# Other sizes for the weight units of the first down product's second half, and a later place for the first S5 factors

## The reference

```python
def swiglu(x, w1, w3, w2):
    return (jax.nn.silu(x @ w1) * (x @ w3)) @ w2

def s5_mixer(u, lam_re, lam_im, log_dt, b_re, b_im, c_re, c_im, d_skip, w_glu, b_glu):
    ...
    bb_re = f_re[..., None] * br - f_im[..., None] * bi
    bb_im = f_re[..., None] * bi + f_im[..., None] * br
    ...

def first_block(...):
    h = x
    for i in range(DEPTH):
        h = layer_norm(DN_ALPHA * h + 0.5 * swiglu(h, ffn_w1[i, 0], ffn_w3[i, 0], ffn_w2[i, 0]),
                       ln_g[i, 0], ln_b[i, 0])
        ...
```

## Time and profile before

| | |
|---|---|
| median of three runs | 2871.54 us |
| profiled execution, its own time | 2872.73 us |
| its span | 2870.9 us |
| TensorE (PE) busy | 2792.7 us, 97% of the span |
| VectorE (DVE) busy | 1769.1 us, 62% |
| GpSimd (POOL) busy | 314.7 us, 11% |
| mean granted TensorE clock | 0.993 |
| TensorE's waits from 255 to 425 us | 1.8 us for VectorE's L966 (once), 0.6 for its L971 (once), 1.3 for its L1832 (once), 0.5 for ScalarE's L618 (twice), 0.4 for ScalarE's L789 (once) |

### The profile page before, as it was taken

The page is one execution under the profiler, slowest core; times in us unless marked ns, Lnnn a source line. Parts: engine busy times, 40 slices in busy tenths (PEclk is TensorE's granted clock), DMA queues, the critical chain, the costliest instruction groups (busy, mean ns, idle before and its releaser), DMA issues.

```text
span 2870.9 us, 34110 instructions
## 1 busy us (share of the span) xinstructions
PE 2792.7 (97%) x13330; PEld 2142.1 (75%) x13330; DVE 1769.1 (62%) x3753; ACT 623.6 (22%) x1360; POOL 314.7 (11%) x301
## 2 busy tenths in 40 slices
PE   9999999999999999999999999999999999999985
PEld 6888887668888877888855577888877766885321
DVE  4788688775755475566348866677356445664223
ACT  1322120022221021221022422222022463001001
POOL 0000020020000100000101430000100473001221
PEclk9999999999999999999999999999999999999998
DMA  4323333112313222133211111232223201257998
GB/s 171 118 103 125 129 125 111 70 59 88 118 67 132 88 88 88 59 118 116 95 71 59 45 59 62 86 118 100 98 74 109 90 16 59 88 238 280 423 425 326
DMA packets 63716, 351.20 MB, mean 122 GB/s; under 512 B 8238, under 2 KB 14510, under 8 KB 24768
## 3 DMA queue, kind: packets, MB, share of 16 engines
q1 hardware_dynamic: 45792, 320.88, 29.1%
q10 hardware_dynamic: 12896, 19.68, 2.0%
q0 software_dynamic: 4864, 8.40, 0.8%
HBM read 339.49 MB, written 14.16 MB: 123 GB/s over the span
## 4 chain that ended last, share of the span: by engine, by line
PE 89%; DVE 4%; SPq 3%; ACT 1%; DMA 1%; issue 1%; ACTq 0%; POOL 0%; DVEq 0%; POOLq 0%
PE bank L944 33%; PE bank L1142 31%; PE bank L542 6%; PE bank L551 5%; SPq L3953 3%; PE bank L4015 2%; PE bank L2836 2%; PE bank L580 2%; PE bank L3441 2%; PE bank L2820 1%; DMA ring<-in_weights 1%; PE bank L4034 1%; PE bank L572 1%; PE bank L685 1%; PE bank L3065 0%
## 5 line engine op out<-in xcount | busy, mean ns | idle before, releaser
L944 PE MATMUL bank<-area,mixed 128*128 128x256 f32 x2264 | 508.4, 379 | 2.4 <-DVE mixed L966 1.8
L944 PEld LDWEIGHTS bank<-area,mixed 128*128 128x128 f32 x2264 | 429.8, 190 | 61.9 <-DVE mixed L966 2.5
L944 PE MATMUL bank<-area,ring 128*128 128x256 f32 x1536 | 346.3, 379 | 0.1
L1142 PE MATMUL bank<-area 128*128 128x256 f32 x1440 | 323.9, 379 | 0.0
L944 PEld LDWEIGHTS bank<-area,ring 128*128 128x128 f32 x1536 | 291.5, 190 | 40.2 <-DVE area L985 0.5
L1142 PEld LDWEIGHTS bank<-area 128*128 128x128 f32 x1440 | 273.7, 190 | 37.1
L1142 PE MATMUL bank<-buf_b,area 128*128 128x256 f32 x1040 | 239.3, 379 | 0.0
L1142 PE MATMUL bank<-buf_a,area 128*128 128x256 f32 x1040 | 239.2, 379 | 0.0
L1142 PEld LDWEIGHTS bank<-buf_b,area 128*128 128x128 f32 x1040 | 197.6, 190 | 27.0 <-issue 0.3
L1142 PEld LDWEIGHTS bank<-buf_a,area 128*128 128x128 f32 x1040 | 197.7, 190 | 26.8
L966 DVE TENSOR_TENSOR mixed<-ring 128x512 f32<-128x512 f32 (+2 forms) x95 | 64.9, 684 | 226.4 <-PE bank L944 226.1
(11 more groups left out here) (645 smaller groups left out, 4345.5 us busy)
## 6 DMA issues: line engine op xcount, KB each, us to landing
ring<-in_weights SPq DMA_DIRECT2D x236, 1024.0 KB, 4.8
area<-in_weights SPq DMA_DIRECT2D x35, 1024.0 KB, 27.9
buf_b<-in_weights SPq DMA_DIRECT2D x10, 1024.0 KB, 26.3
buf_a<-in_weights SPq DMA_DIRECT2D x8, 1024.0 KB, 24.6
const<-in_weights SPq DMA_DIRECT2D x5, 1024.0 KB, 27.9
norm<-in_weights SPq DMA_DIRECT2D x4, 1024.0 KB, 22.4
mixed<-in_weights SPq DMA_DIRECT2D x4, 1024.0 KB, 26.4
area<-area ACTq DMA_DIRECT2D x20, 128.0 KB, 2.4
```

What stands on the lines that cost most here:

```text
L944: mm = pe.e.matmul(b, w[:, k * P:(k + 1) * P], x(INPUT_OF[p], unit.lo + k), start=(unit.key, BANK_OF[p]) not in begun, stop=unit.last and ...
L1142: mm = pe.e.matmul(out[:, half * H:(half + 1) * H], weights[:, at:at + P], x(name, d), start=fresh and half == 0 and d == 0, stop=half == ...
```

## The change

`SECOND_FIRST` = 1 is new. In the second half of the first down (products 4 to 7), the five pairs are cut into a unit of one pair and then one of four, in place of four and then one. `groups_of` gives the cut, `square` lays the weights out in that order, `place_pieces` starts a new block behind the unit of one pair, and `Unit` and `plan_units` read the cut from `groups_of`. A product of the second half takes two blocks of the ring as before. Besides this, `vector_s5_b(ve, 0)` moves from ahead of the loop to behind the weight sums of unit (0, 1).

```diff
--- before.py
+++ after.py
@@ -65,7 +65,7 @@
 ROUTED = 8 + NEXP
 EARLY_QUERIES = 1
 GROUP = 4
-FIRST_PAIRS = 6
+FIRST_PAIRS, SECOND_FIRST = 6, 1
 WIDE_FFN, WIDE_GROUPS = (0, 1, 2, 3), 5
 SQUARE = ("ffn0_wide", "ffn1_wide", "ffn2_wide", "ffn3_wide", "ffn0_down", "ab_hu", "ffn1_down", "ffn2_down", "ffn3_down",
           "ab_out", "ple0_gate", "c_out", "ple1_gate", "b_merge", "b_out",
@@ -90,15 +90,20 @@
     return ((k * P, P),)
 
 
-def square(name, index, outs, ins, rows=whole, cols=whole):
+def groups_of(n, first=GROUP):
+
+    return [(0, min(first, n))] + [(lo, min(lo + GROUP, n)) for lo in range(first, n, GROUP)]
+
+
+def square(name, index, outs, ins, rows=whole, cols=whole, first_group=GROUP):
 
 
     products = []
     for first, second in outs:
         pieces = []
-        for lo in range(0, len(ins), GROUP):
+        for lo, hi in groups_of(len(ins), first_group):
             for out, side in ((first, 0), (second, 0), (first, 1), (second, 1)):
-                pieces += [(name, index, rows(pair[side]), cols(out)) for pair in ins[lo:lo + GROUP]]
+                pieces += [(name, index, rows(pair[side]), cols(out)) for pair in ins[lo:hi]]
         products.append(pieces)
     return products
 
@@ -125,7 +130,7 @@
     wide = [(2 * c + 1, 2 * c) for c in range(KF // 2)]
     outs = [(2 * c + 1, 2 * c) for c in range(KD // 2)]
     if (layer, i) == (0, 0):
-        return square("ffn_w2", (layer, i), outs, wide[:FIRST_PAIRS]) + square("ffn_w2", (layer, i), outs, wide[FIRST_PAIRS:])
+        return square("ffn_w2", (layer, i), outs, wide[:FIRST_PAIRS]) + square("ffn_w2", (layer, i), outs, wide[FIRST_PAIRS:], first_group=SECOND_FIRST)
     return square("ffn_w2", (layer, i), outs, wide)
 
 
@@ -236,8 +241,11 @@
 def place_pieces(plan):
 
 
-    places, block, col, last = [], 0, 0, (None, 0)
+    places, block, col, last, n_taken = [], 0, 0, (None, 0), 0
     for (name, m), piece in in_order(plan):
+        n_taken = n_taken + 1 if last == (name, m) else 0
+        if name == "ffn0_down" and m >= KD // 2 and n_taken == 4 * SECOND_FIRST:
+            block, col = block + 1, 0
         if col and (name.startswith("moe") and name != last[0] or name in SQUARE and
                     ((name, m) != last and col + sum(map(width_of, plan[name][m])) > BLOCK or name != last[0])):
             block, col = block + 1, 0
@@ -839,9 +847,10 @@
     class Unit:
 
 
-        def __init__(self, key, n, name, m, at):
+        def __init__(self, key, n, name, m, at, first_group):
             self.key, self.n, self.index = key, n, len(units)
-            self.lo, self.size = n * GROUP, min(GROUP, len(plan[name][m]) // 4 - n * GROUP)
+            self.lo, hi = groups_of(len(plan[name][m]) // 4, first_group)[n]
+            self.size = hi - self.lo
             self.last = self.lo + self.size == len(plan[name][m]) // 4
             self.block, self.col = places[first_place[name, m] + at]
             assert places[first_place[name, m] + at + 4 * self.size - 1][0] == self.block
@@ -913,10 +922,10 @@
             return first_copied, counts_before(i)[1] + n + 1
         return first_copied, counts_before(f"ffn{i}")[1] + N_COPIES * WIDE_GROUPS + n + 1
 
-    def plan_units(key, name, m):
+    def plan_units(key, name, m, first_group=GROUP):
         at = 0
-        for n in range(-(-len(plan[name][m]) // (4 * GROUP))):
-            unit = Unit(key, n, name, m, at)
+        for n in range(len(groups_of(len(plan[name][m]) // 4, first_group))):
+            unit = Unit(key, n, name, m, at, first_group)
             at += 4 * unit.size
 
     def plan_part(unit, p):
@@ -1033,7 +1042,7 @@
 
     def plan_first_down(aside):
         for n in range(2 * DOWN):
-            plan_units(down_key(0, n), "ffn0_down", n)
+            plan_units(down_key(0, n), "ffn0_down", n, GROUP if n < DOWN else SECOND_FIRST)
         for n in range(FIRST_LEAD):
             for part_of_k in range(2):
                 for p in (1, 2):
@@ -1792,7 +1801,6 @@
         for c in range(2, FIRST_PAIRS):
             first_mixed(ve, c)
         vector_s5_start(ve)
-        vector_s5_b(ve, 0)
         u2, u3, u4 = first_u2, first_u3, first_u4
         for n in range(2 * DOWN):
             key, c, final = down_key(0, n), n % DOWN, n >= DOWN
@@ -1801,7 +1809,7 @@
                 done(down_key(0, DOWN - 1), 1, 6)
                 first_mixed(ve, FIRST_PAIRS + GROUP)
             vector_mix(ve, unit_of[key, 1].index)
-            if 0 < n < STEPS:
+            if n < STEPS:
                 vector_s5_b(ve, n)
             for k, side in ASIDE_C.get((n, 0), ()):
                 vector_s5_c(ve, k, side)
```

## The result

The change runs in 2878.02 us (median; 2876.70 to 2881.11), the kernel before on the same chip in 2871.97 (2870.84 to 2873.97). The ratio is 1.0022, with a 95% interval of [1.0014, 1.0029]: 6.05 us or 0.21% slower. The interval leaves out 1, and the difference lies close to the 5.7 us that the forecast took as the least to be told from no change. The forecast was 2876.4 in 2872.8 to 2879.2. One run of the change, at 2977.87 us with a granted clock of 0.943, was in a slower state and is left out of its range and of the ratio.

What follows compares the result with a forecast made beforehand. TensorE, holding 89% of the chain that ended last, was taken to bound the kernel. Terms -1.3 + 5.3 + 2.0 - 1.7 - 0.4 + 1.0 = +4.9 us on 2871.5 gave 2876.4 us, range 2872.8 to 2879.2.

Steps and rivals of the forecast that it cites:

- The signs named for it: Changed profile: no idle in unit (0, 1), 3.9 us wait at (4, 0), two near 1 us for S4, spread 2 us behind.
- factor 0 moved: Units (0, 1) and (1, 0): 2.0 us hole goes, 0.65 wait for S2 comes; net -1.3 us, bounds -2.0 and 0.
- unit (4, 0), waits: Unit (4, 0): TensorE waits for VectorE's sums, losing 6.9 us in place of 1.6; +5.3 us, bounds +2.3 and +6.
- clock dip there: Unit (4, 0): the thin stretch of work likely lowers the granted clock; taken as +1.0 us, between nothing and 1.7.
- meetings with GpSimd: Units (6, 0) and (7, 0): narrow S2 and S4 fall under GpSimd operations, 1.0 us each; +2.0 us, bounds 0 and +2.5.
- end of the last product: Last unit, now four pairs: the norm's first spread comes about 2.1 us behind, not 3.8; -1.7 us, bounds -2.1 and -1.
- no dip behind it: Behind the last product: thin stretch half as long, so the clock dip may go; -0.4 us, bounds 0 and -1.
- first edit: Factor 0 behind the sums of unit (0, 1): removes a 2.0 us hole, adds a 0.65 wait; net -1.3 us.
- clock rival: Half rate reaches past unit (4, 0) over full work: +1.7 to +3.4 in place of +1.0, 2877 to 2879 us; chance 0.27.
- last sign of being wrong: The forecast is wrong if the clock stays down for long behind unit (4, 0), the first of the single-pair units.
- case of the sum: All terms hold as summed: +4.9 us, 2876.4 us, 0.17% slower; chance 0.46.
- Nothing later takes it up: Behind the changed stretch: the chain runs on through TensorE and SP's loads move along, so the +4.9 us stays.

Runs made afterwards that it cites:

- filled: Against the changed kernel, matmuls that nobody reads fill TensorE's waits at unit (4, 0) ahead of parts 5, 7 and 6; 2875.31 us, ratio 1.0013.
- sums first: Against the changed kernel, S2 and S4 of the next unit stand ahead of L1840, whose result starts GpSimd, in products 4 to 6; 2875.95 us, 1.0013.
- both: Against the changed kernel, input sums of pairs 6 to 9 moved away, and S2 and S4 put ahead of the result that starts GpSimd; 2868.01 us, 0.9986.
- second run: The changed kernel measured once more without any edit, on the chip of three other follow-up kernels; 2878.90 us, 1.0025 against the kernel before.

## Why the prediction was right, and where its terms were off

**The place and the mechanism held.** The loss is at unit (4, 0), whose S1 comes late because VectorE has the sixteen input sums ahead of it; taking them away took the loss away. The signs named for it came: no wait in unit (0, 1), a long wait for S1 at (4, 0) and shorter ones behind it, waits for S4 at (6, 0) and (7, 0), the spread 2.12 behind the products.

| term | predicted | measured | by |
|---|---|---|---|
| factor 0 moved | -1.3 | -1.3 | profile after, and alone |
| unit (4, 0), waits | +5.3 | +5.4 | 10.0 us filled, less 3.02, less 1.6 before |
| clock dip there | +1.0 | +1.6 | filled against the change |
| meetings with GpSimd | +2.0 | +1.5 | sums first |
| end of the last product | -1.7 | -1.7 | 2.12 against 3.82 |
| no dip behind it | -0.4 | -0.4 | 6.43 from spread to next stage, 6.81 before |
| sum | +4.9 | +5.1 | first matmul of the next stage: +5.35 |

Of the 0.25 between the last two, 0.15 has nothing to do with the change: the row ahead of the first edit's place stood at 280.80 in place of 280.65, so unit (4, 0) starts 1.15 earlier than in the earlier trace rows, not 1.31. The other 0.1 has no place in these rows. That the sum comes so near is in part luck: the dip was taken 0.6 too small and the meetings 0.5 too large. And the median lies 1.6 above the forecast: 0.4 because the kernel before measured 2871.97 and not 2871.5, and 1.15 because the difference was 6.05 and not 4.9; of these 1.15 the stretch accounts for 0.45.

**The first edit** went as said, to 0.14 us in the new wait (0.51, forecast 0.65).

**The dip was mis-sized.** I had taken +1.0 between "ends inside the wait" and "all over full work". The clock didn't fall during the wait for S1: it was 1.00 up to 348 and half from about 348.7 to 355.5 (worked out from the means 0.67 and 0.62 of two levels), twice as long as in the earlier trace rows. The first half of this cost nothing, since the parts hung on VectorE; the second lay over parts 6 and 3 and the transposes. The clock rival's condition, half rate past the end of (4, 0), is thus what happened, at 1.6 us just short of its lowest price (1.7), and the low clock reached over most of the transposes and not over the raw parts of (4, 1). So the last sign of being wrong, a clock that stays down behind the unit, came in part: it stayed down for 1.6 us more. The median of 2878.0 lies in its 2877 to 2879: the case of the sum, held likelier, got the place and the waits, and the rival with 0.27 the clock.

**The meetings were over-sized** by 0.2 each. I had priced GpSimd's second operation at 1.7, from the earlier trace rows. Behind the narrow S2 it took 1.32, so S4 ended earlier, and TensorE waited 0.57 in place of 1.0.

**The end of the last product** came out as forecast: VectorE's results end earlier against TensorE's part 3 of four pairs, as the forecast had it. The -0.4 for the clock behind it was measured too, but that the new units are its cause isn't shown: the kernel with only the factors moved has the old thin stretch, and its clock stayed at 1.00 there. The dip stood in one of the two profiles with the old units and in none of the eight with new ones.

**"Nothing later takes it up" was too simple.** From the first matmul of the next stage to the product near 2178 us every kernel but one takes 1752.9 us (1753.2 in "sums first"), so nothing is taken up there. Behind it the clock decides. At the wait of 2.77 us for L2113 (2.80 in "both") it fell in seven of the ten profiles (the change, its second run, and five of the others) and kept 1.00 in three (before, both, filled); the stage from there to the matmuls of the routing (128x48) takes 441.95 to 442.00 us with the dip and 440.24 to 440.28 without. That is 1.7 us that a kernel gets or doesn't by the execution, and what is left from the routing to the end of the span spreads further (255.7 to 259.4 us). With the stretch, this makes the two profiled executions differ by 8.4 us in span where the medians differ by 6.05. Whether unprofiled runs of the change meet such dips more often than those of the kernel before, and whether that is the 0.7 us (in the second run 2.4) that the medians show beyond the stretch, and part of the 3.6 of the filled kernel, is open: no run here separates it.

## What to carry to other kernels

Where units on one engine need operands that another engine prepares in order, the raw work at a unit's head is the cover for the first prepared operand: before making a unit smaller, look at what stands ahead of that operand on the other engine, because a jam that four pairs hide (1.6 us lost) one pair does not (7.0). The same new cut is slower or faster by what stands around it: with the jam moved into idle time and two sums put ahead of the result that wakes GpSimd, the kernel is 3.7 us faster than the one before, 1.0 of which the factor's new place gave by itself. How much the old cut would gain with the jam moved, up to its 1.6 us at (4, 0), was not run. Price a broken stretch of TensorE with the clock behind it too, and set a yardstick inside the trace beside the medians, since dips elsewhere come and go by more than a us.

## What was not expected of the hardware

- Where the clock falls is not tied to the wait alone. With the same wait for S1 (3.75 to 3.76 us) it fell about 0.4 us behind the start of part 5 in the change (0.67 in the window from 348), 0.7 behind it with only the new units (0.96 from 348), and at the very start of part 5 in the change's second run (0.97 from 346); these times are worked out from two levels, 1.00 and 0.50. The Trainium skill, page TensorE: Matmul & The Clock Gate, part 1 (the HAM clock gate), says that the gate's watch runs free of the program, so that the same kernel may see it act at other places from run to run. The traces agree, by these places and by the next two: with the same wait of 2.77 us (2.80 in one) it fell in seven of ten profiles, and behind the last product, with the old units, it fell before and not where only the factors had moved.
- VectorE and GpSimd, side by side, change each other's durations in both directions: VectorE's sum of 128 columns took 1.36 us in place of 0.28 under GpSimd, and GpSimd's 128x512 addition took 1.71 to 1.72 us where a 512-wide addition of VectorE had come in between it and the one before, and 1.32 where a narrow sum and a read of a bank had (row 386.25).
